# A transformer chain on one Trainium2 core: units side by side behind the first output projection, residuals in PSUM, rotary halves by DMA, an earlier start of stick-breaking

## What is computed

```
first block:
  x = x + 0.5 * rms_norm(swiglu(rms_norm(x)), g)            # ff1, 2816 hidden features
  x = x + rms_norm(hybrid_mixer(rms_norm(x)), g)            # rotary q and k, differential and sparse
                                                            # attention, then w_out (out1)
  x = x + 0.5 * rms_norm(swiglu(rms_norm(x)), g)            # ff2
second block, layers A and B:
  A: gated short convolution beside cross attention to a memory of 256 tokens, w_o, swiglu
  kv = rms_norm(x) @ w_kv_shared
  B: stick-breaking attention (12 heads) beside cross attention, w_o, swiglu
out = rms_norm(x)
partial_rope: of each head's 64 features the first 16 turn: [x1*cos - x2*sin, x2*cos + x1*sin], 8 each
```

## Time and profile before

| | |
|---|---|
| median of 3 runs | 2310.27 us (2309.74 to 2311.41) |
| the profiled execution | 2309.9 us, its span 2307.8 us |
| busy in the span: TensorE, DVE, ACT, POOL | 97%, 41%, 36%, 42% |
| mean granted clock of TensorE | 0.986 of full |
| DMA read from HBM | 198.54 MB, 87 GB/s |

### The profile page before, as it was taken

One profiled execution on the slowest core, in us unless ns is written; L12 is line 12 of the kernel. 1 busy time (PEld: TensorE's weight loads), 2 busy tenths in 40 slices (PEclk: granted clock), 3 DMA queues, 4 the chain that ended last, 5 costly groups with the idle time before them and its releaser, 6 DMA issues.

```text
span 2307.8 us, 28179 instructions
## 1 busy us (share of the span) xinstructions
PE 2234.9 (97%) x10366; PEld 1771.7 (77%) x10366; DVE 944.0 (41%) x1289; ACT 823.8 (36%) x1362; POOL 974.6 (42%) x435
## 2 busy tenths in 40 slices
PE   8999999999998999999999999999999889999997
PEld 6888887875556788888777888888877568888886
DVE  3211346356874411234675311134552653111345
ACT  4222335324873322223532422223342654222222
POOL 4444444553003544444443454444443434544442
PEclk9999999999998999999999999999999899999999
DMA  5222232432001322323232232222222002322221
GB/s 188 91 95 105 91 111 89 127 110 74 1 1 55 110 91 91 104 97 109 73 110 73 82 118 91 101 100 91 91 91 75 17 1 92 109 100 100 91 93 70
DMA packets 29799, 202.66 MB, mean 88 GB/s; under 512 B 3360, under 2 KB 4000, under 8 KB 6048
## 3 DMA queue, kind: packets, MB, share of 16 engines
q1 hardware_dynamic: 28800, 198.55, 24.5%
q10 hardware_dynamic: 928, 3.14, 0.4%
HBM read 198.54 MB, written 2.10 MB: 87 GB/s over the span
## 4 chain that ended last, share of the span: by engine, by line
PE 69%; DVE 4%; ACT 1%; issue 1%; POOL 1%; DVEq 0%; ACTq 0%; POOLq 0%
PE PS L946 20%; PE PS L948 20%; PE PS L947 20%; PE PS L1377 1%; PE PS L1238 1%; PE PS L1197 1%; PE PS L1269 1%; DVE NMAX L1667 1%; PE PS L1361 1%; PE PS L1389 1%; DVE ACC L1434 1%; PE PS L1017 0%; POOL X L479 0%; PE PS L1220 0%; DVE TMP L1514 0%
## 5 line engine op out<-in xcount | busy, mean ns | idle before, releaser
L454 POOL TENSOR_TENSOR WL<-RAW,WH 128x1024 fp32r<-128x1024 f32 x368 | 908.5, 2473 | 1234.4 <-ACT WH L521 1234.4
L946 PE MATMUL PS<-XH,WH 128*128 128x512 f32 (+1 forms) x2200 | 865.9, 394 | 28.9 <-DVE XL L1426 19.8
L948 PE MATMUL PS<-XH,WL 128*128 128x512 f32 (+1 forms) x2200 | 853.2, 388 | 0.0
L947 PE MATMUL PS<-XL,WH 128*128 128x512 f32 (+1 forms) x2200 | 852.8, 388 | 0.0
L521 ACT ACTIVATE WH<-RAW 128x1024 fp32r<-128x1024 f32 x368 | 388.1, 1059 | 1255.4 <-PE PS L948 1211.2
L946 PEld LDWEIGHTS PS<-XH,WH 128*128 128x128 f32 x2200 | 415.4, 189 | 125.1 <-issue 27.6
L947 PEld LDWEIGHTS PS<-XL,WH 128*128 128x128 f32 x2200 | 415.7, 189 | 86.6 <-issue 4.1
L948 PEld LDWEIGHTS PS<-XH,WL 128*128 128x128 f32 x2200 | 415.3, 189 | 84.8
L946 PE MATMUL PS<-HH,WH 128*128 128x512 f32 x672 | 261.4, 389 | 0.0
L947 PE MATMUL PS<-HL,WH 128*128 128x512 f32 x672 | 261.4, 389 | 0.0
L948 PE MATMUL PS<-HH,WL 128*128 128x512 f32 x672 | 261.4, 389 | 0.0
(11 more groups left out here) (194 smaller groups left out, 1558.2 us busy)
## 6 DMA issues: line engine op xcount, KB each, us to landing
RAW<-wstream SPq DMA_DIRECT2D x183, 1024.0 KB, 4.8
X<-xT SPq DMA_DIRECT2D x4, 512.0 KB, 9.0
WORK<-memT ACTq DMA_DIRECT2D x2, 1024.0 KB, 5.4
outT<-WORK SPq DMA_DIRECT2D x8, 256.0 KB, 2.1
RAW<-wstream SPq DMA_DIRECT2D x2, 512.0 KB, 6.3
PB<-WORK ACTq DMA_DIRECT2D x8, 127.8 KB, 2.3
CST<-consts SPq DMA_DIRECT2D x1, 912.0 KB, 10.6
WORK<-constsb SPq DMA_DIRECT2D x1, 256.0 KB, 12.4
```

The source lines that it names most:

```text
L454: pool.tensor_tensor(WL[:, s, :, :].rearrange("p a b -> p (a b)"), RAW[:, s, :], WH[:, s, :, :].rearrange("p a b -> p (a b)").bitcast(F), ...
L946: pe.matmul(o, wh, xh, start=start, stop=False)
L947: pe.matmul(o, wh, xl, start=False, stop=False)
L948: return pe.matmul(o, wl, xh, start=False, stop=stop)
```

## The change

- `post_mem` and `pre_norm_mem` take the place of `post` and `pre_norm` behind `down0` and `down1`: banks 5 to 7 are finished first and copied (`YC`), the memory units use banks 5 and 6, DVE puts gain·RSTD·y and then X + that into a PSUM bank (`XBANK`), ACT makes XH from it and copies it back to X one chunk later, DVE makes XL from it. POOL updates nothing there; TensorE waits for the copies back before it writes those banks.
- `ff2` (behind `out1`): three units side by side, `ssq` after the fourth; two refills of the ring move into the pre-norm's squares.
- every `gate_up`: the fifth and sixth unit go to banks 4 and 5, without a wait for `gu_free`.
- `mix_post` and `final`: the eighth square isn't added; TensorE multiplies ACC and the last SQ by ones, into the same bank. In `post_norm` the refills stand after the squares.
- rotary: the PERM matmul goes; ACT issues four DMAs of 8 partitions for each unit, SQ to LT; SIN carries the sign; `rope` waits for `rotated`.
- stick-breaking: the scores of steps 0 to 3 stand before the last `kv` unit, and their work on DVE and ACT inside that unit; kv's last four units use banks 2, 3, 6 and 7; the last transposes are made in place; POOL's first 8 splits of sums stand before two weight splits.
- constants PERM and MASK go, `LT` is set to zero at the start.

The core of the diff:

```diff
-X_ON_DVE = {"down0": (0, 2, 4, 6), "out1": (0,), "down1": (0, 2, 4, 6)}
+X_ON_DVE = {"down0": tuple(range(KC)), "out1": (0,), "down1": tuple(range(KC))}
+Y_ORDER = {"down0": (5, 6, 7, 0, 1, 2, 3, 4), "down1": (5, 6, 7, 0, 1, 2, 3, 4)}
+XBANK = (0, 1, 2, 3, 4, 7, 5, 6)
-SIDE = {"ff1": 2, "proj1": 2, "ff2": 2, "projA": 2, "ffnA": 2, "projB": 2, "kv": 2, "ffnB": 2}
-SSQ_AT = {"ff1": 3, "proj1": 3, "ff2": 3, "projA": 3, "ffnA": 3, "projB": 3, "ffnB": 3}
+SIDE = {"ff1": 2, "proj1": 2, "ff2": 3, "projA": 2, "ffnA": 2, "projB": 2, "kv": 2, "ffnB": 2}
+SSQ_AT = {"ff1": 3, "proj1": 3, "ff2": 4, "projA": 3, "ffnA": 3, "projB": 3, "ffnB": 3}
+SB_AHEAD = 4
...
+            split_units(0, U0["gu1"] + POOL_X_AT)
+            update_x("out1")
+            split_units(U0["gu1"] + POOL_X_AT, U0["outB"] + 2)
+            low_softplus(0, 8)
+            split_units(U0["outB"] + 2, U0["outB"] + RING)
+            low_softplus(8, len(SBSTEPS))
             split_units(U0["outB"] + RING, NLOAD)
...
+            def pre_norm_mem(name, part, mem):
...
+                for k in range(KC):
+                    if k == 0:
+                        refill(mem, 1, 0)
+                    if k == 2:
+                        refill(mem, 1, 1)
+                    if k == 4:
+                        unit(U0[mem] + 3)
+                    x_wait(act, part, k)
+                    act.activation(XH[:, k, :], PS[:, XBANK[k], :], ACT.Copy, scale=gain(name, k)
+                                   ).then_inc(xh_ready, 1)
+                    if k:
+                        copy_back(k - 1)
+                copy_back(KC - 1)
+                refill(mem, 2, 2)
+                squares(name, lambda k: X[:, k, :], KC, lambda k: act.wait_ge(xc_done, n + k + 1))
+                for y in JOBS[mem][2:]:
+                    turn(y)
+                rstd(name, KC, 7)
...
             def post_norm(name, part):
 
                 def ready(k):
-                    if part.startswith("out"):
-                        refill(part, 1, k)
                     if k == 0:
-                        act.wait_ge(y0_done, POSTS.index(part) + 1)
-                    elif part.startswith("down"):
+                        act.wait_ge(y0_done, 1)
+                    else:
                         y_wait(act, part, k)
 
+                squares(name, lambda k: PS[:, k, :] if k else Y0[:, :], KC, ready,
+                        lambda k: refill(part, 1, k))
+                rstd(name, KC, 0)
...
+            def rotate(x):
+
+                act.wait_ge(taken, x["t"] + 1)
+                for a in (0, DH):
+                    for b in (0, 8):
+                        act.dma_start(LT[a + b:a + b + 8, x["c"] % 2, :],
+                                      SQ[a + 8 - b:a + 16 - b, x["f"] % 2, :]).then_inc(rotated[x["c"] % 2], 16)
+
...
+                    if part == "kv" and n == len(jobs) - 1:
+                        turn(jobs[n - 2])
+                        for t in range(SB_AHEAD):
+                            sb_exp_ln(t)
                     unit(x["u"])
...
+                    if x["kind"] in ROTARY:
+                        rotate(x)
...
-            pre_norm("ff2_pre", x_normed("out1"))
+            pre_norm("ff2_pre", x_normed("out1"), after=lambda k: refill("gu1", 1, k // 2) if k in (1, 3) else None)
...
+                    if k == 0 and stage == "ff2" and bank == 2:
+                        pe.wait_ge(y_scaled, KC * POSTS.index("out1") + 3)
+                    if k == 0 and copied is not None:
+                        pe.wait_ge(xc_done, copied + bank + 1)
...
+                    pe.wait_ge(sq_added, ADD0[name] + KC - 1 - (name in LAST_ALONE))
                     src = ACC[:, :]
+                if name in LAST_ALONE:
+                    pe.matmul(PS[:, bank, :], ONES, src, start=True, stop=False)
+                    pe.wait_ge(sq_ready, SQ0[name] + KC)
+                    pe.matmul(PS[:, bank, :], ONES, SQ[:, (KC - 1) % 2, :], start=False,
+                              stop=True).then_inc(ssq_done, 1)
+                    return
...
                 if SSQ_AT[stage] == 4:
                     ssq(PRE[l], 7)
-                with pe.Fori(0, FC // 2 - 1) as i:
-                    for f in range(2):
-                        pe.wait_ge(gu_free, i * 2 + (FC * l + f + 1))
+                for j in range(4, 6):
+                    features(u0 + j, j, stage)
+                with pe.Fori(0, (FC - 3) // 2) as i:
+                    for f in range(3, 5):
+                        pe.wait_ge(gu_free, i * 2 + (FC * l + f - 1))
...
-                if x["kind"] in ROTARY:
-                    mm = pe.matmul(PS[:, 4 + f % 2, :], PERM, SQ[:, f % 2, :], start=True, stop=True)
...
+                        if part == "kv" and i == len(jobs) - 1:
+                            pe.wait_ge(taken, jobs[i - 2]["t"] + 1)
+                            for t in range(0, SB_AHEAD, 2):
+                                sb_pair(t)
                         features(x["u"], x["bank"], stage, first=x["n"] == 0,
                                  release=part in XH_USERS and i == len(jobs) - 1)
...
-                    if k >= 2:
-                        low(stage, nxt, k - 2, X[:, k - 2, :])
-                    if mem and 1 <= k <= 4:
-                        take_mem(JOBS[mem][k - 1], k - 1)
+                    if k == 1 or k >= 3:
+                        low(stage, nxt, max(k - 2, 0), X[:, max(k - 2, 0), :])
...
+            def post_mem(name, part, stage, nxt, mem):
...
+                        dve.scalar_tensor_tensor(bank, y, gain(name, k), RSTD[:, :],
+                                                 ALU.mult, ALU.mult).then_inc(y_scaled, 1)
+                        dve.wait_ge(y_scaled, n + k + 1)
+                        dve.tensor_tensor(bank, X[:, k, :], bank, ALU.add).then_inc(xd_ready, 1)
+                    if k >= 1:
+                        low(stage, nxt, k - 1, PS[:, XBANK[k - 1], :])
+                    if k in (2, 4):
+                        for j in (k - 2, k - 1):
+                            take_mem(JOBS[mem][j], j, JOBS[mem][k - 1])
...
-                dve.wait_ge(flipped, f + 1)
-                chain(dve.tensor_tensor(TMP[:, 1, :], SIN, PS[:, 4 + f % 2, :], ALU.mult))
+                dve.wait_ge(rotated[x["c"] % 2], 64 * ((x["c"] + 1) // 2))
+                chain(dve.tensor_tensor(TMP[:, 1, :], SIN, LT[:, x["c"] % 2, :], ALU.mult))
...
+                    if last and part == "kv":
+                        for t in range(SB_AHEAD):
+                            sb_step(t)
```

More of the change, by code:

```diff
@@ L106, in bank_of @@
         return dict(slot=slot, bank=n % 4, free=t - 3 if n >= 4 else 0, after=False)
+    if part == "kv" and slot >= 16:
+        return dict(slot=slot, bank=slot - (14 if slot < 18 else 12), free=0, after=True)
     if slot >= 18:
@@ L470, in split_units, with update_x @@
                     split_unit(v)
-            def update_x(part, units=()):
-                units = list(units)
+            def update_x(part):
                 for k in range(KC):
@@ L491, in low_softplus @@
                                        ALU.subtract).then_inc(sb_lo, 1)
-            first = 0
-            for part, mem in (("down0", "mem0"), ("out1", None), ("down1", "mem1")):
-                if mem:
-                    u = U0[mem] + RING
-                    split_units(first, u)
-                    update_x(part, (u, u + 1))
-                    first = u + 2
-                else:
-                    split_units(first, U0["gu1"] + POOL_X_AT)
-                    update_x(part)
-                    first = U0["gu1"] + POOL_X_AT
-            split_units(first, U0["outB"] + RING)
-            low_softplus()
+            split_units(0, U0["gu1"] + POOL_X_AT)
[4 more added lines that the diff above has]
+            low_softplus(8, len(SBSTEPS))
             split_units(U0["outB"] + RING, NLOAD)
@@ L589, in pre_norm, with copy_back @@
                 rstd(name, KC, 7)
+            def pre_norm_mem(name, part, mem):
+                n = KC * POSTS_MEM.index(mem)
+                def copy_back(k):
+                    act.wait_ge(xn_ready, KC * XN["proj1" if mem == "mem0" else "projA"] + k + 1)
+                    act.activation(X[:, k, :], PS[:, XBANK[k], :], ACT.Copy).then_inc(xc_done, 1)
+                for k in range(KC):
[16 more added lines that the diff above has]
+                rstd(name, KC, 7)
@@ L877, in _ @@
             tables()
-            post_norm("ff1_post", "down0")
-            pre_norm("mix_pre", x_normed("down0", "mem0"), middle=lambda: refill("mem0", 2, 2),
-                     late=lambda: [turn(y) for y in JOBS["mem0"][2:]])
+            post_norm_mem("ff1_post", "down0")
+            pre_norm_mem("mix_pre", "down0", "mem0")
             project("proj1")
@@ L963, in features, with side_by_side @@
                 mm.then_inc(unit_done, 1)
[L965 removed]
+            def side_by_side(units, stage, alone=0, join=0, copied=None):
```

(5 more changed lines are left out.)

386 lines of the change are left out of this document (204 added, 182 removed).

## The result

The changed kernel takes 2328.7 us (median, 2327.2 to 2330.4) beside 2310.7 of the kernel before (2309.7 to 2311.4): ratio 1.008, 95% interval 1.007 to 1.009. It is 18 us slower where I predicted 11 faster, and lies 20.7 us above the upper end of my range.

A forecast was written before the change was run, and what follows sets the result against it. TensorE, busy 2234.9 of 2307.8 us, bounds the kernel; gains come from its 73 us not busy and matmuls saved. +8.9 - 3.0 - 3.0 - 10.7 - 3.0 + 0 = -10.8: 2299.5 beside the median, range 2288 to 2308.

The forecast's parts named there:

- Rotary halves by DMA: proj1: 12 PERM matmuls of 0.93 us leave TensorE, four DMAs a unit come on ACT's queue; gain 10.7 (3 to 13).
- DVE's cycle: Rotary units in the dk/w1k stretch: take, issues, landing, multiply and add last 6.3 to 7.7 us against 6.8 a pair.
- issues and landing: Rotary DMAs of one unit: three issues 1.9 us in DVE's cycle, then 2.3 for the landing.
- multiply and add 1.4 to 2.8: DVE's two rotary operations behind the landing, 1.4 to 2.8 us of its cycle.
- TensorE has four banks: Rotary units in proj1: DVE slips at most 1 us a pair, and TensorE has four banks.
- Rival C: All 14 rotary units slowed, with landings about 5 us on average, cycle 8.7 against 6.8: +15, 2314.5; chance 0.08.
- Rival B: Rotary DMAs meet the weight stream in the dk units, DVE's cycle 10 to 11: +4 to +10, about 2306; chance 0.15.
- Three abreast: Behind out1: TensorE waits for POOL's third split behind seven additions, and the squares are late; costs 8.9 us (7 to 11).
- PSUM residuals: Behind down0 and down1: chunks at 2.05 us with PSUM operands; gain 3.0 at each (0 to 4.5 each).
- Stick-breaking: At the last kv unit: first four scores go in front, their work runs under a unit; gain 3 (0 to 6).
- The end: Last norm: ACC matmul starts at 2295.8, end 2298.0 to 2298.9 against 2298.3; 0 (-0.4 to +0.6).
- Two more in other banks: Units 4 and 5 in banks 4 and 5 hide the RSTD chain behind 10.9 us of work; gain 0.

The follow-up runs named there:

- perm_back: Changed kernel with the rotation by a permutation matmul on TensorE put back for each of 14 units: 2312.7 us, ratio to before 1.001.
- defer_rope: Changed kernel, four transfers a unit kept, with VectorE's rotation put off by one unit: 2303.3 us, ratio to before 0.997.
- sin_in_psum: Changed kernel with the table of sines copied once to a PSUM bank, so the product reads PSUM and SBUF: 2311.2 us, ratio 1.001.
- two_back: Changed kernel with two units abreast behind out1 instead of three, and the fifth and sixth units' roundings back behind the squares: 2315.2 us, ratio 1.003.
- only_squares: Changed kernel with both the permutation back on TensorE and two units abreast behind out1: 2298.5 us, ratio 0.995.

## Why the prediction was wrong, step by step

**Rotary halves by DMA: predicted -10.7, measured +17.2 in proj1 (16.0 in medians, by perm_back).** The removal was right: 12 x 0.93 = 11.2, and defer_rope, with a wait at the first softmax that is 2.7 longer in sum, still has the stage 9.7 shorter than before; for that wait, at the last landing, I had 0.5 (-0.6 to 3). The step that failed is "DVE's cycle ... is 6.3 to 7.7: it slips at most 1 us a pair, and TensorE has four banks". A cycle above TensorE's 6.8 was priced at nothing for TensorE, and the cycle was 10.0 in the mean of the first four, not 7.7 at most. Its terms one by one, predicted and measured in the cycle from 468.24 to 478.48, and behind that in the first five units:
- take 0.7: 0.7.
- issues and landing 1.9 + 2.3 = 4.2: 3.98, right in sum. In the five units 4.0 to 7.0, mean 4.9, with one late landing.
- "multiply and add 1.4 to 2.8": 5.6. This was the mis-sized term, by 2.8 over its upper end here; in the five units 2.8 to 5.6, mean 3.9, so 1.1 over. I had the rule and the row that agrees with it (2.52 beside a split) in the next paragraph, applied it to the product only, and wrote that it adds 1.8 "on DVE, and TensorE's sum stays". It applies to the final sum as well, an instruction with two SBUF inputs that takes 2.77 here against 1.2 before (472.77 in the trace of before). The Trainium skill (SBUF — State Buffer, Who interferes with whom) says that a VectorE instruction with two SBUF inputs contends with a GpSimd instruction that reads SBUF, and one with at most one doesn't; the trace agrees, 2.5 (median) against 0.69 with one input in PSUM. Over all 14 units the product grew most, from 9.6 to 29.0 us in sum, and the sum, which had met splits before too, from 18.8 to 24.1. With the 1.8 that I had myself the cycle is 8.1 to 9.5, already above 6.8; measured, four cycles alone lose 13.0 (40.2 less 27.2).
- "TensorE has four banks": true, and beside the point. TensorE's link to DVE was not the banks but the copy of the hidden sums and `low_b`, both behind DVE's chain.
- Nor is the contention a chance meeting. ACT rounds as soon as it has issued, POOL splits as soon as ACT has rounded, and the landing falls into that split: ten of the 14 products took 2.1 to 2.9 us, all of the first five among them.

Rival C (slower, 14 units, a cycle of 8.7) had the right place and sign with a chance of 0.08; its 2314.5 is still 14 below the measured time. It was made to depend on a landing of 5 us in the mean; in the cycle above the product started 2.0 behind the start of the last issue, and DVE's own operations made the cycle. Rival B (a set meets the weight stream) did happen, once in the changed kernel: the second set's last issue was at 460.4, SP had issued a weight transfer 0.2 earlier, and the product started 5.05 behind that last issue. The traces of the seven kernels with the rotation in this place bear it out: in all seven sets where a weight transfer was issued 0.2 us before the last issue, the product started 5.0 to 5.1 behind it, where it was issued over 3.7 us before or only behind the last issue, 2.0 to 2.3, and at 3.0 to 3.4 before, 2.6 to 3.1. No run took the weight stream away. In the changed kernel B is 3.0 us of the 13.0 that the first four cycles lose; sin_in_psum, with two such landings, loses nothing against before, so B alone did not make the loss.

**Three abreast: predicted +8.9, measured +16.3 in its stage** (13.5 in medians, by two_back). Mechanism right, size short. TensorE's restart lies 18.1 behind RSTD (752.09 to 770.16) where I had 17.1 (754.5 less 737.4); the three units took 18.8 (predicted 19.1). From restart to ones I had 25.3 and it was 28.0: the adds behind the late squares, beside POOL's splits, took 8.5 for six, not 7.6, and TensorE waited 3.4 for them. Behind that pause TensorE's matmuls started 0.43 apart, as in the first matmuls of the restart (the granted clock from 798 to 803 is 0.66 in the mean, most of it at 1.2 GHz): ten of them took 4.3 us (798.73 to 802.99), 2.0 more than at 0.227. The stage interval also counts that the ones of out1 themselves come 2.5 earlier (0.23 behind the start of the last product's matmul, before 2.75), which is the last square's gain, so 13.8 is the like-for-like figure, beside the 13.5 of the medians.

**PSUM residuals: predicted -3.0 and -3.0, measured -4.3 and -4.7**, in every one of the 13 traces with the change. VectorE writing to PSUM took the reads' price here, 0.75 and 0.69 a chunk, which I had taken without a row; a chunk takes 2.05 as predicted (378.69 to 380.74). What I sized too late was ACT's last copy back (395.3, not 397.3), so squares and ones came 1.3 earlier. The wait for `WL` before the third unit was 1.4 (predicted 1.8). These two gains are read from the intervals; no run put the old residuals back.

**Stick-breaking: predicted -3, measured -2.8.** At the first running sum the changed kernel is 4.5 ahead of the one before, 2.4 of it by the early scores. What reaches the end of the stage is not shown to be theirs: without them it is as short, within what the clock does from kernel to kernel. So that the number fits is in part luck.

**The end: predicted 0, measured -0.5** (from outB's ones to the end of the span 358.2 before, 357.7 after; in the other runs with the change 357.7 to 359.4, so 0.5 is inside what they differ by). "Two more in other banks", 0: no run tests it alone. The last square's gain at out1, which I had inside the +8.9 as 2.6, was 2.6: from the last product's matmul to RSTD 5.57 us before, 2.96 after.

**Sum.** Predicted -10.8; the intervals sum to +21.7, less 1.1 outside them: the span's 20.6 (the profiled execution is 1.5 above the median). Of the error of 32.5 in the intervals and the prediction's sum the rotary part is 27.9 and three abreast 7.4; the PSUM residuals take 3.0 back.

## What to carry to other kernels

An operation moved off the engine that bounds the kernel is free only if what it feeds is off the chain too: write down the cycle of every engine that it enters, with contended prices for each instruction with two SBUF inputs if another engine's work is released by the same event, and compare it with the pace of the engine that bounds. If the new step has latency, let the consumer do one unit of other work first: here a few moved lines turned an 18 us loss into a 7 us gain. And when units start abreast, move their preparation ahead of everything that now stands before it; one number was worth 11.5 us.

## What the runs showed of the hardware that I had not expected

The granted clock fell in mix1 in some kernels whose code there is the same. Table by stretches, 40 us of mix1, before and then only_squares (busy time of each engine, granted clock, DMA share, GB/s):

```profile
620.00:660.00 40.00, 37.32 (x283) 20.50 (x278) 34.15 (x102) 33.75 (x116) 0.00 (x0) 1.00 0.00 1
```

```profile
616.00:656.00 40.00, 38.36 (x233) 20.95 (x232) 27.24 (x84) 27.53 (x98) 0.00 (x0) 0.74 0.00 1
```

50 matmuls fewer in the same time, at a mean of 0.74 (part of the stretch at 1.2 GHz, the rest at 2.4): that is the 168.0 of only_squares against 160.6 to 163.4 elsewhere, up to 7 us in a stretch of mix1 that no edit touched. With two levels, 0.74 means that some 21 of the 40 us ran at 1.2 GHz. The changed kernel has 0.91 there, some 7 us, and loses 2.5, which hides the last square's 2.5: in the runs with 1.00 there the stage is 160.6, before 163.2. In stick-breaking the same goes for defer_rope (192.2, granted clock 0.90 in its middle 70 us) against only_squares (185.1, 0.98). What decides it from kernel to kernel stays open.

A transfer of 8 rows took ACT's queue 0.63 us to issue, four of them 2.6, and the rounding behind them started when the fourth was out (471.67). From the start of the last issue to DVE's product pass 2.0 us, but 5.0 where SP had just issued a weight transfer.
